# Expert feed-forward of a two-layer decoder: down units placed between the next round's gate and up units, blocks of 1024 columns, down rows two to a partition

## The reference, cut to what matters

```python
def moe_swiglu(h, w_router, w_gate, w_up, w_down):
    t = h.reshape(N, D)
    logits = (t @ w_router).astype(jnp.float32)
    top_v, top_e = lax.top_k(logits, TOP_K)
    gates = jax.nn.softmax(top_v, axis=-1)
    ...
    def expert_block(args):
        xb, e = args
        return (jax.nn.silu(xb @ w_gate[e]) * (xb @ w_up[e])) @ w_down[e]
    ...
```

## Time and profile before

| | us |
|---|---|
| median of 3 runs | 1470.59 (1470.44 to 1470.79) |
| the profiled execution | 1470.37 |
| its span, first to last instruction | 1468.8 |

### The profile page before, as it was taken

How to read it: one execution, slowest core, us unless ns; L and a number is a source line. 1 busy time by engine, 2 the same in 40 slices (tenths; PEclk the granted TensorE clock), 3 DMA queues, 4 the chain that set the end, 5 groups by cost and what they waited for, 6 DMA issues and landing times.

```text
span 1468.8 us, 18954 instructions
## 1 busy us (share of the span) xinstructions
PE 1411.0 (96%) x6739; PEld 1149.5 (78%) x6739; DVE 1215.0 (83%) x1504; ACT 1008.2 (69%) x1287; POOL 124.9 (9%) x175
## 2 busy tenths in 40 slices
PE   8999999999999999999999889999889999989997
PEld 6768888888988888888887678887668887667776
DVE  7775644554886689999999998999998999999897
ACT  7566444444524578877878887878887787888676
POOL 1000400000333084000000000000000000001000
PEclk9999999999999999999999999999999999999999
DMA  9515897554633569999999999999999999999993
GB/s 336 181 59 172 292 411 256 193 172 143 201 117 114 172 242 377 409 377 386 401 376 375 401 395 371 397 398 376 394 401 370 390 405 377 387 408 384 390 399 130
DMA packets 199230, 460.32 MB, mean 313 GB/s; under 512 B 9193, under 2 KB 18465, under 8 KB 199137
## 3 DMA queue, kind: packets, MB, share of 16 engines
q1 hardware_dynamic: 190240, 433.09, 80.2%
q0 software_dynamic: 7168, 25.43, 4.8%
q10 hardware_dynamic: 1728, 0.59, 0.2%
HBM read 438.37 MB, written 20.71 MB: 313 GB/s over the span
## 4 chain that ended last, share of the span: by engine, by line
PE 67%; DMA 11%; DVE 10%; ACT 3%; issue 2%; SPq 0%; DVEq 0%; ACTq 0%
PE bank L1696 20%; PE bank L1698 20%; PE bank L1697 20%; DMA raw<-in_w_gate_moe_dram 4%; DVE w_lo L1067 4%; DVE w_lo L1062 4%; DMA raw<-in_w_down_moe_dram 4%; DMA raw<-in_w_up_moe_dram 3%; ACT w_hi L673 2%; PE bank L1890 1%; PE bank L2061 1%; ACT w_hi L678 1%; PE bank L1702 1%; PE bank L1703 1%; PE bank L1717 0%
## 5 line engine op out<-in xcount | busy, mean ns | idle before, releaser
L673 ACT ACTIVATE w_hi<-raw 128x1024 fp32r<-128x1024 f32 x411 | 436.7, 1062 | 372.6 <-PE bank L1698 291.4
L1062 DVE TENSOR_TENSOR w_lo<-raw,w_hi 128x1024 fp32r<-128x1024 f32 x411 | 504.9, 1228 | 171.0 <-ACT w_hi L673 169.8
L1067 DVE TENSOR_TENSOR w_lo<-raw,w_hi 128x1024 fp32r<-128x1024 f32 x411 | 505.6, 1230 | 0.7 <-ACT w_hi L678 0.7
L1696 PE MATMUL bank<-w_hi,t_hi 128*128 128x512 f32 (+1 forms) x1144 | 450.1, 393 | 5.8 <-DVE w_lo L1062 4.3
L1697 PE MATMUL bank<-w_lo,t_hi 128*128 128x512 f32 (+1 forms) x1144 | 444.3, 388 | 0.0
L678 ACT ACTIVATE w_hi<-raw 128x1024 fp32r<-128x1024 f32 x411 | 430.1, 1046 | 0.9 <-DMA raw<-in_w_in_attn_dram 0.9
L1698 PE MATMUL bank<-w_hi,t_hi 128*128 128x512 f32 x728 | 284.0, 390 | 0.0
L1696 PEld LDWEIGHTS bank<-w_hi,t_hi 128*128 128x128 f32 x1144 | 215.2, 188 | 55.6 <-issue 6.9
L1697 PEld LDWEIGHTS bank<-w_lo,t_hi 128*128 128x128 f32 x1144 | 215.4, 188 | 43.6 <-issue 1.0
L1696 PE MATMUL bank<-w_hi,h_hi 128*128 128x512 f32 x408 | 163.7, 401 | 0.6 <-DVE h_lo L1291 0.5
L1698 PE MATMUL bank<-w_hi,t_lo 128*128 128x512 f32 (+1 forms) x416 | 160.4, 386 | 0.0
(11 more groups left out here) (329 smaller groups left out, 1253.9 us busy)
## 6 DMA issues: line engine op xcount, KB each, us to landing
raw<-in_w_gate_moe_dram SPq DMA_DIRECT2D x112, 1024.0 KB, 13.7
raw<-in_w_up_moe_dram SPq DMA_DIRECT2D x112, 1024.0 KB, 12.2
raw<-in_w_down_moe_dram SPq DMA_DIRECT2D x112, 1024.0 KB, 13.5
raw<-in_w_in_rec_dram SPq DMA_DIRECT2D x16, 1024.0 KB, 5.7
raw<-in_w_gate_dense_dram SPq DMA_DIRECT2D x14, 1024.0 KB, 5.4
raw<-in_w_up_dense_dram SPq DMA_DIRECT2D x14, 1024.0 KB, 6.8
raw<-in_w_down_dense_dram SPq DMA_DIRECT2D x14, 1024.0 KB, 4.9
raw<-in_w_in_attn_dram SPq DMA_DIRECT2D x8, 1024.0 KB, 14.9
```

Of the source, the lines that this page charges most:

```text
L673: act.activation(w_hi[:, (u - 1) % SPL, half], raw[:, r, half], ACT.Copy).then_inc(hi_half, 1)
L1062: dve.tensor_tensor(w_lo[:, s, half], raw[:, r, half], w_hi[:, s, half].bitcast(F32), ALU.subtract).then_inc(lo_half, 1)
L1067: dve.tensor_tensor(w_lo[:, s, half], raw[:, r, half], w_hi[:, s, half].bitcast(F32), ALU.subtract).then_inc(lo_done, 1)
L1696: pe.matmul(o, lh, rh, start=start, stop=False)
```

## The change

**Blocks.** Six of seven gate and up blocks become three double blocks of 1024 columns (`WIDE` = 3): a unit is then 256 rows x 1024 columns, in runs of 4096 bytes, and four of them make the gate or up part of a double block, in two banks. The seventh block (4 of 28 units) stays as it was. A down unit is still 256 rows x 1024 columns, but partition p holds rows 2p and 2p+1, which lie side by side in DRAM: runs of 8192 bytes. The hidden block is transposed with the matching stride.

**Order.** A *phase* is the down part of one expert and the gate and up part of the next: pairs of gate or up units 0 to 13 in order, and behind each pair from the fourth on (`LAG` = 3) one down unit, so that 11 of 14 stand between pairs and 3 at the end. It begins with 28 gate and up units of the first expert alone, then come seven phases, then the last expert's 14 down units alone. The places' order becomes 0, 5, 1, (loop) 2, 6, 3, 7, 4: six phases have one small and one other expert, the third (the loop's) has two that are not small. The rows of the second expert go to `t_lo`.

**Behind the last phase.** The result of place 7, a small one, is now ready when that phase ends, right ahead of the 14 units that stand alone. Its store, the four gathers and the four additions come in that last part: DVE waits for `y_back` after its second hidden block there.

```diff
-AHEAD_OF_LOOP = ((0, False), (1, False), (5, True), (2, False), (6, True))
-LOOP_PLACE, SMALL_PLACE, LAST_PLACE = 3, 7, 4
+BEFORE_LOOP = ((0, False), (5, True), (1, False))
+LOOP_PLACE = 2
+BEHIND_LOOP = ((6, True), (3, False), (7, True), (4, False))
+LAST_PLACE = 4
+GU = 4 * FB
+DOWN = FCH // 2
+LAG = 3
+WIDE = 3
+def behind_pair(pair):
+    return 2 * (pair + 1) + max(0, pair - LAG)
...
-            dv = w_down_moe[0].rearrange("e (u k p) n -> p e u k n", p=P, k=2)
+            dv = w_down_moe[0].rearrange("e (u p k) n -> p e u k n", p=P, k=2)
...
-                b, h = u // 4, u % 2
-                return (gv, uv)[u % 4 // 2][:, bass.ds(e, 1), 4 * h:4 * h + 4, b * BLK:(b + 1) * BLK]
+                if u >= GU:
+                    return dv[:, bass.ds(e, 1), u - GU]
+                if u >= 8 * WIDE:
+                    h = u % 2
+                    return (gv, uv)[u % 4 // 2][:, bass.ds(e, 1), 4 * h:4 * h + 4, WIDE * 2 * BLK:]
+                w, h = u // 8, u % 4
+                return (gv, uv)[u % 8 // 4][:, bass.ds(e, 1), 2 * h:2 * h + 2, w * 2 * BLK:(w + 1) * 2 * BLK]
+            def load_phase(e_down, e_next):
+                at = U0 + GU
+                for pair in range(2 * FB):
+                    load_pair(e_next, pair, at)
+                    at += 2
+                    if pair >= LAG:
+                        load(expert_unit(GU + pair - LAG, e_down), at)
+                        at += 1
+                for j in range(2 * FB - LAG, DOWN):
+                    load(expert_unit(GU + j, e_down), at)
+                    at += 1
...
+            hidden_lo(0)
+            for g in range(2, 7):
+                split_to(start + 2 * (g - 2) + 2 + SPL)
+                hidden_lo(g + 1)
+                if g == 2:
+                    dve.wait_ge(y_back, 16 * 2 * TT)
+                if g < 6:
+                    r, t = (g - 2) // 2, g % 2
+                    link(dve.scalar_tensor_tensor(X[:, t, :], back[t][r], row_f[:, 3, t, r:r + 1], X[:, t, :],
+                                                  ALU.mult, ALU.add))
+            split_to(start + DOWN)
...
+                    if at == LAG:
+                        open_bank(YB)
+                        open_bank(YB + 1)
+                    if at >= LAG:
+                        down_unit(at - LAG, small_down)
...
+            phase(True, False, t_hi, last=True)
+            expert_transposes(1, into=1)
+            open_bank(YB)
+            open_bank(YB + 1)
```

More of the change, by code:

```diff
@@ new lines, in left_results, with phase @@
+            def left_results():
+                act.wait_ge(y_stored, n.step("stored", 16))
+                wait_units(start + FFN_UNITS, YB, YB + 1)
+                act.activation(ybuf[:, 0:BLK], bank[YB][:], ACT.Copy).then_inc(free[YB], 1)
+                n.count["half"] = 2 * (start + AHEAD)
+            def phase(small, last=False):
+                for w in range(WIDE + 1):
+                    if w == 0:
+                        hidden(0, small)
+                        hidden(1, small)
+                    elif w < WIDE:
+                        hidden(2 * w, small)
+                    gate_rows(w, start + behind_pair(4 * w + 1 if w < WIDE else 4 * w))
+                    if w:
+                        hidden(2 * w + 1 if w < WIDE else 2 * w, small)
+                    if last and w == 1:
@@ L970, in _ @@
-            for _, small in AHEAD_OF_LOOP:
-                expert(small, False)
-                left_results()
+                if last:
+                    split_to(start + FFN_UNITS - 2 + SPL)
+                    act.wait_ge(unit_done, unit_at(start + FFN_UNITS - 2))
+                    hidden_hi(1)
+                else:
+                    split_to(start + behind_pair(2 * FB - 1) + SPL)
+                    act.wait_ge(unit_done, unit_at(start + behind_pair(2 * FB - 1)))
+                    gather_hi(t_hi)
@@ L973, in _ @@
+                split_to(start + FFN_UNITS + AHEAD)
+                left_results()
+            act.activation(epsc[:, 2:3], epsc[:, 0:1], ACT.Silu)
+            for w in range(WIDE):
+                gate_rows(w, U0 + 8 * w + 4)
+            gate_rows(WIDE, U0 + 8 * WIDE + 2)
+            gather_hi(t_lo)
+            split_to(start + AHEAD)
+            for _, small in BEFORE_LOOP[:-1]:
+                phase(small)
                 n.rounds += 1
@@ new lines, in phase @@
+            def phase(small, last=False):
+                for g in range(FB):
+                    hidden(g, small)
+                    if g % 2 or g == FB - 1:
+                        up_rows(g // 2, start + behind_pair(min(2 * g + 1, 2 * FB - 1)))
+                    if last and g == 3:
+                        saw(TR)
+                if last:
+                    split_to(start + FFN_UNITS - 2 + SPL)
+                    hidden_lo(1)
+                else:
+                    gather_lo(t_hi)
+                split_to(start + FFN_UNITS + AHEAD)
+                right_results()
@@ L1628, in _ @@
+            for w in range(WIDE):
+                up_rows(w, U0 + 8 * w + 8)
+            split_to(U0 + 8 * WIDE + 2 + SPL)
+            gather_lo(t_lo)
+            up_rows(WIDE, U0 + GU)
+            for _, small in BEFORE_LOOP[:-1]:
+                phase(small)
                 n.rounds += 1
```

444 lines of the change are left out of this document (232 added, 212 removed).

## The result

The changed kernel takes **1455.21 us** (median of four runs, 1453.9 to 1455.45) against 1470.51 for the kernel before, measured beside it: ratio 0.9894, 95% interval 0.9877 to 0.9911. The forecast was 1457 with a range of 1435 to 1477. The profiled execution spans 1453.5 us. PE has the same 6739 instructions as before, the packets fall from 199230 to 135743 for the same bytes. The first fence is the page of after; the earlier trace rows has the page of before.

What follows compares the result with a forecast made beforehand. Loads were taken as the bound on the average, PE and DVE within 7%. PE reaches the lone down units at 1381.7; 62.9 gives 1444.6, 10.8 follows to 1455.4, device overhead makes 1457 us; range 1435 to 1477.

Steps and rivals of the forecast that it cites:

- Gate and up runs: Gate and up units in seven phases: 4096-byte runs land in 2.56 us instead of 2.71, 26.7 us saved.
- down units lying in one piece: Rival for the loads: one-piece rows, not run length, made down units quicker; 1487 us, slower; chance 10%.
- Down runs: 98 down units in 8192-byte runs: between 0 and 7.8 us saved, 3.7 taken.
- The phases: Six mixed phases: loads need 111.7 us, DVE 108.8, PE 104.5; the third phase needs 117.2 of PE.
- closeness: Seven phases: loss from loads, DVE and PE being nearly full together, 0.3 us each, 2 us in all.
- Rival 1: Mixed phases: engines, not loads, bound them, at 114.2 us instead of 111.7; 1470 us; chance 20%.
- PE idle 7 us: Sign of being right: a mixed phase of 111 to 113 us with PE idle 7 of them.
- What the loads still cost: Mixed phases: loads stay the bound, 3 us over DVE; their lead of up to 6 us is used up after phase three.
- T: Time when PE reaches the lone down units: 1416.4 - 26.7 - 3.7 - 6.3 + 2 = 1381.7 us.
- the traffic moved away: Last small result's store and four gathers, 2.6 MB, now lie behind the last phase's loads: 6.3 us less.
- The lone down part: Last 14 down units: gathers at T + 32.5, then 28.4 and 2.0; 62.9 us against 41.8, 21 given back.
- Rival 2: Lone down part: the end costs nothing, gathers arriving before PE has used up its five units; 1436 us; chance 12%.

Runs made afterwards that it cites:

- order-only kernel: Changed kernel with the new order kept, but gate and up units in 2048-byte runs and down units in 4096-byte runs; 1485.6 us.
- half-fetched kernel: Changed kernel with the down units of the mixed phases fetching only the first of their two rows, the 14 lone ones whole; 1447.7 us.
- the first kernel: Changed kernel with down runs of 4096 bytes again instead of 8192; 1459.32 us.
- The experiment: Changed kernel with later share additions, result copied before the third advance split, and ACT copying one-hot rows before the hidden block; 1436.78 us.
- the early copy: Changed kernel with later share additions, and the last small result copied out of its banks before the third advance split; 1438.27 us.

## Why the prediction was right, step by step

1. **Gate and up runs**. Forecast 26.7; the kernels that differ in them alone differ by 26.3. That the pace comes from run length and not from down units lying in one piece, which the prediction gave 10% against, is settled by the order-only kernel: with short runs back it takes 1485.6, where the prediction's price for loads without the gain was 1487. The Trainium skill, "DMA: Bandwidth & Descriptors", section "Where 436 GB/s comes from", has reads bound at about 358 GB/s; 390 and 405 in these phases disagree, as in the prediction.
2. **Down runs.** Forecast 3.7, meant as the middle between 0 and 7.8 (which is 3.9). Taken apart: the loads gained nearly all of it, 2.49 us a unit for the 2.48 that the line through the other two run lengths gives, and the time showed 4.1 in after's order and 3.5 in before's. So the term came out by luck: not a half-effect on the loads, as assumed, but a full one of which the engines let half through. The 4096 bytes of the Trainium skill, "DMA: Bandwidth & Descriptors", section "SWDGE vs HWDGE vs iDMA", by which the term would be 0, bounded nothing here: runs of 8192 bytes were moved whole (after's packets of 8192 bytes or more are 135743 - 121312 = 14431) and were faster.
3. **The phases**. Forecast 111.7 us for a mixed phase and 117.2 for the third; measured 110.9 on the average and 116.9. Behind the loads the prediction had DVE at 108.8, and 0.3 more for closeness: 109.1. With half the down bytes, where ACT never waits for a landing, the six mixed phases take 107.6 to 111.1 us, 109.6 on the average. But neither engine is full in them: of after's 109.3 in the fourth, PE is busy 108.1 and DVE 107.0. What bounds the phases at this pace is not shown. Rival 1 had two halves. Its price, 114.2 us a phase, is out; its mechanism, engines that bound the phases and not the loads, holds for all mixed phases but the sixth and a part of the second. The prediction also looked for PE idle 7 us in a mixed phase; the rows show 1.2 to 4.8. Its 104.5 us of PE is a count of products at 0.227 us and never shows as busy time.
4. **What the loads still cost.** This step was wrong, without harm to the sum. The forecast had the loads 3 us over DVE in each mixed phase. The half-fetched kernel says 6.8 us over all seven, 5.8 of them in one. The prediction had seen that the loads run up to 6 us ahead in phase 3, and yet kept the loads as the bound of the phases behind it; the lead covers two of them whole. That a mixed phase came near 111.7 all the same is in part luck: the first takes 111.0 for another reason than the loads, and so does the last (point 6).
5. **T.** Forecast 1381.7, measured 1380.55. In the order-only kernel T is 1411.3, where 1416.4 - 6.3 + 2 gives 1412.1, so the traffic moved away and the price of closeness are right as a pair (nothing separates them). From there the long gate and up runs take 25.1 us off T (1386.2 in the first kernel), and the long down runs 5.6, for 26.7 and 3.7.
6. **A step that was missing.** The last unit of the last phase lands at 1369.0 us, 11.5 before T. ACT never waits for a landing in that phase, so loads don't bound it. What adds to it is a stop at 1321 to 1328 us: PE waits for ACT to have copied the transposed one-hot rows, which ACT does only behind the hidden block of that place, and ACT then waits for PE. PE and ACT of after:

```profile
1324.11 0.49 PE L1801 MATMUL bank<-w_hi,h_hi 128*128 128x512 f32 x1 [2.74 <-ACT ST L1041]
```

```profile
1327.52 1.06 ACT L742 ACTIVATE w_hi<-raw 128x1024 fp32r<-128x1024 f32 x1 [3.53 <-PE bank L1802]
```

   The experiment prices it at 3.0 us of the phase, and the clock that falls with it costs some 1.5 more. The forecast has no term for this; it came out because it had the loads too late in the same phase (111.7 us forecast, 111.9 measured). That is luck.
7. **The lone down part**. Forecast 62.9, measured 62.1, term by term: banks free for PE at T + 4.6, in fact DVE's copy ends at T + 6.0 and PE starts at T + 6.2; gathers at T + 32.5, in fact T + 30.1, since from the copy to the last landing it took 24.1 us for the 27.9 forecast (227 GB/s were moved from 1387 to 1399 us, where before it was 375 to 397 beside the same chain); from there to the last product 30.4 (28.4 and 2.0), in fact 32.0. PE stood from T + 24 instead of T + 19: it began later, and its five units took 17.8 us and not 14, with the clock at 0.50 for the first 3.4 us and 0.90 for the rest. Two misses of about 2 us cancel. The part is the same 62 us (61.8 to 62.2) in the three other kernels that leave the additions where after has them, whatever their loads. That the wait, with what is queued behind it, was the cause and not loads or PE, is shown by moving the additions: 12.4 us of the 20.3 given back; the early copy took 3.3 more out of the part.
8. **Behind it** the last 10.8 us are 10.85, and the time is 1.7 over the span. Rival 2, at 1436, needed the gathers before T + 19; they were 11 us too late. It takes three moves in the program to get there: 1436.8.

## What to carry to other kernels

Price an interleaving of stages at both ends: what it evens out in the middle is worth only what the scarcest resource lets through, and the work that used to hide a round trip through memory at the end has moved away. Where the bound alternates between loads and engines, only a part of a gain at the loads gets through: of some 7 us saved on the down loads, 3.5 and 4.1 here. A phase that something else bounds fills the ring of loads, and that lead must be carried through the next phases, one by one. Behind a wait for a round trip, ask what else is queued on that engine: here the additions could wait, and the splits behind them could not.

## What the runs showed of the hardware that I had not expected

- The time of one run grows along a straight line with its length, up to 8192 bytes. By the trace's records of single packets of after (598 to 1380 us), the medians are 87 ns for 2048 bytes, 162 for 4096 and 314 for 8192; a unit of 1.0486 MB takes 2.71, 2.56 and 2.49 us. The last doubling still brings half of what the first brought.
- A wait of PE can cost more than its length. Busy by stretch of after, right behind its waits of 5.55 and 8.80 us:

```profile
1386.75:1390.20 3.45, 3.45 (x8) 2.77 (x9) 0.37 (x1) 0.00 (x0) 0.62 (x2) 0.50 1.01 406
...
1413.36:1416.80 3.44, 3.44 (x8) 2.76 (x9) 3.44 (x4) 0.00 (x0) 0.00 (x0) 0.50 0.35 81
```

  The granted clock is 0.50, which is the 1.2 GHz level, and eight products take 3.4 us instead of 1.8. After shorter waits it went either way. The same wait of 2.74 us for `ST` was followed by a mean clock of 0.57 in after and 1.00 in the kernel with the early copy (the first and second fence; the third is that kernel's wait):

```profile
1324.10:1328.10 4.00, 3.99 (x13) 3.18 (x14) 2.38 (x4) 0.58 (x1) 0.00 (x0) 0.57 1.01 413
```

```profile
1320.00:1332.00 12.00, 9.26 (x43) 7.40 (x42) 10.26 (x12) 7.78 (x10) 0.00 (x0) 1.00 1.02 413
```

```profile
1324.66 0.49 PE L1822 MATMUL bank<-w_hi,h_hi 128*128 128x512 f32 x1 [2.74 <-ACT ST L1042]
```

  What decides between the two is open; no run was made for it. In the last phase it is 1.5 us (111.8 and 110.3). Repeated times of one kernel spread by as much or more, 1437.8 to 1440.1 with the early copy and 1446.7 to 1449.0 half-fetched; whether such waits make that spread is not shown.
